# Odd mixer's gates and running maxima on quarters of the rows, MLP norms by an all-ones matmul, block-attention scores in another order

## What is computed

```python
x = first_block(x, ...)            # modulated rmsnorm, window attention + block ("moba") attention, MLP
for layer in range(2):
    h = _rmsnorm(x, mix_norm_g[layer])
    x = x + (_even_mixer(h) if layer == 0 else _odd_mixer(h))
    h = _rmsnorm(x, mlp_norm_g[layer])
    x = x + _sqrelu_mlp(h, mlp_w1[layer], mlp_w2[layer])   # relu(h @ w1)**2 @ w2

def _odd_mixer(h, ...):            # w_in is (1024, 3080): 512 q, 512 k, 1024 v, 1024 og, 8 gates
    p = h @ w_in
    qk = silu(causal_conv(p[..., :1024]))
    i_pre, f_pre = gates[..., :4] + i_b, gates[..., 4:] + f_b
    hc = _mlstm(q, k, v, i_pre, f_pre)      # 4 heads, logf = log_sigmoid(f_pre), cumulative sums,
    ...                                     # running maxima of i - cumsum(logf) per head and token
```

## Time and profile before

| | us |
|---|---|
| median of 3 runs | 1875.85 (1875.34 to 1876.64) |
| the profiled execution | 1876.47 |
| its span, first to last instruction | 1874.7 |
| PE busy | 1841.8 (98%) |
| DVE busy | 961.6 (51%) |
| ACT busy | 733.8 (39%) |

### The profile page before, as it was taken

How to read it: one execution, slowest core, us unless ns; L and a number is a source line. 1 busy time by engine, 2 the same in 40 slices (tenths; PEclk the granted TensorE clock), 3 DMA queues, 4 the chain that set the end, 5 groups by cost and what they waited for, 6 DMA issues and landing times.

```text
span 1874.7 us, 21068 instructions
## 1 busy us (share of the span) xinstructions
PE 1841.8 (98%) x8632; PEld 1497.2 (80%) x8632; DVE 961.6 (51%) x1389; ACT 733.8 (39%) x1043; POOL 39.1 (2%) x75
## 2 busy tenths in 40 slices
PE   5999999999999999999999999999999999999999
PEld 4787788788888888877888888888876788888887
DVE  7487546543434355767543434345735554444343
ACT  4355532332323243467442323243445443323231
POOL 0100000000000000001000000000011000000000
PEclk9999999899999999999999999999999999999999
DMA  8365543222222223211222222222220223222222
GB/s 330 117 198 186 168 163 120 88 101 90 101 90 101 97 95 118 79 35 46 90 91 101 90 101 101 90 102 90 90 79 36 78 90 111 92 101 91 101 90 79
DMA packets 55120, 197.65 MB, mean 105 GB/s; under 512 B 6400, under 2 KB 6656, under 8 KB 55024
## 3 DMA queue, kind: packets, MB, share of 16 engines
q1 hardware_dynamic: 52272, 188.24, 28.2%
q0 software_dynamic: 2320, 7.31, 1.4%
q10 hardware_dynamic: 432, 0.74, 0.1%
HBM read 194.13 MB, written 2.14 MB: 105 GB/s over the span
## 4 chain that ended last, share of the span: by engine, by line
PE 94%; DVE 4%; ACT 1%; issue 0%; DMA 0%; ACTq 0%; DVEq 0%
PE ps L314 27%; PE ps L316 26%; PE ps L315 26%; PE ps L350 2%; PE ps L351 2%; PE ps L352 2%; PE ps L439 1%; PE ps L815 1%; DVE ARENA L1384 1%; PE ps L722 1%; PE ps L368 1%; PE ps L682 1%; PE ps L520 0%; PE ps L802 0%; PE ps L494 0%
## 5 line engine op out<-in xcount | busy, mean ns | idle before, releaser
L314 PE MATMUL ps<-R0h,WH 128*128 128x512 f32 x1176 | 461.9, 393 | 5.9 <-DVE R0l L1436 4.6
L918 ACT ACTIVATE WH<-RAW 128x1024 fp32r<-128x1024 f32 x299 | 313.9, 1052 | 392.6 <-PE ps L316 337.7
L1377 DVE TENSOR_TENSOR WL<-RAW,WH 128x1024 fp32r<-128x1024 f32 x299 | 365.4, 1225 | 191.3 <-ACT WH L918 187.4
L315 PE MATMUL ps<-R0l,WH 128*128 128x512 f32 x1176 | 458.8, 390 | 0.0
L316 PE MATMUL ps<-R0h,WL 128*128 128x512 f32 x1176 | 458.8, 390 | 0.0
L314 PE MATMUL ps<-R1h,WH 128*128 128x512 f32 x1064 | 417.7, 393 | 3.0 <-DVE R1l L1588 2.5
L316 PE MATMUL ps<-R1h,WL 128*128 128x512 f32 x1064 | 414.7, 390 | 0.0
L315 PE MATMUL ps<-R1l,WH 128*128 128x512 f32 x1064 | 414.7, 390 | 0.0
L314 PEld LDWEIGHTS ps<-R0h,WH 128*128 128x128 f32 x1176 | 221.4, 188 | 57.6 <-DVE R0l L1436 6.4
L316 PEld LDWEIGHTS ps<-R0h,WL 128*128 128x128 f32 x1176 | 221.4, 188 | 46.4
L315 PEld LDWEIGHTS ps<-R0l,WH 128*128 128x128 f32 x1176 | 221.5, 188 | 45.3
(11 more groups left out here) (283 smaller groups left out, 1435.8 us busy)
## 6 DMA issues: line engine op xcount, KB each, us to landing
RAW<-in_W SPq DMA_DIRECT2D x339, 512.0 KB, 3.2
ARENA<-in_W SPq DMA_DIRECT2D x12, 512.0 KB, 13.2
XT<-in_X SPq DMA_DIRECT2D x4, 512.0 KB, 9.2
ARENA<-bias_scratch POOLq DMA_DIRECT2D x8, 256.0 KB, 4.3
XT<-in_X POOLq DMA_DIRECT2D x8, 256.0 KB, 3.5
out_x<-XT SPq DMA_DIRECT2D x8, 256.0 KB, 2.0
ARENA<-bias_scratch POOLq DMA_DIRECT2D x8, 128.0 KB, 3.6
con<-in_CON POOLq DMA_DIRECT2D x1, 578.0 KB, 4.3
```

Of the source, the lines that this page charges most:

```text
L314: e.matmul(ps(b), wh, hi, start=first, stop=False)
L315: e.matmul(ps(b), wh, lo, start=False, stop=False)
L918: e.activation(slot(n)[0], src, ACT.Copy).then_inc(sem["w_hi"])
L1377: e.tensor_tensor(wl, src, r32(wh), ALU.subtract).then_inc(sem["w_lo"])
```

## The change

- **Gates.** The chunk og8 goes (24 matmuls, one load of 512 KB, one split). The gate weights become 8 x 32 columns of `par` (wg), which grows from 164 to 421 columns, and are multiplied once by the norm's gain on DVE (`gate_weights`, one 128x256 operation before the residual sums of the even mixer). `gate_columns` multiplies them in plain fp32 with XT: 8 matmuls with 128 rows, 32 columns, 512 moving columns; k-step k writes the column quarter k mod 4 of bank 0. ACT copies the bank. `gate_sum`, one gemm later, adds the quarters with two 128x128 matmuls against 0/1 matrices, so that four copies of the 4 gate rows lie at partitions 0, 32, 64, 96. LI, FX and T2 are worked on with 128 partitions.
- **Maxima.** `gate_rows` takes head h from partitions 32h..32h+3, all four heads in a row, behind the v-gemm part that stood between them.
- **Pair of the odd mixer.** It now is the first two q/k chunks.
- **MLP norms (m1, m2).** `sums_wide` multiplies SQ by a 128x128 matrix of ones, 512 moving columns, at k-step 3. ACT takes the root of the 128x512 bank, DVE the reciprocal of 128x512. `bring` is gone there. One `hi` and one `lo` stand before the root, one behind.
- **Scores of the second kind.** Order of tiles (e,i): before 0,3 1,3 0,2 1,2 0,1 1,0 0,0 1,1; now 0,3 1,3 0,1 1,2 0,2 1,0 0,0 1,1, and the last waits for the third score instead of the fifth.

```diff
@@ scores, heads 4 to 7
-                    for b in (3, 5):
+                    for b in (7, 5):
                         open_bank(b)
+                    score(j, 0, 1)
+                    score(j, 1, 2)
+                    open_bank(3)
                     score(j, 0, 2)
-                    score(j, 1, 2)
-                    open_bank(7)
-                    score(j, 0, 1)
                     score(j, 1, 0)
                     score(j, 0, 0)
-                    e.wait_ge(sem["qk"], 8 * j + 5)
+                    e.wait_ge(sem["qk"], 8 * j + 3)
                     score(j, 1, 1)
@@ PE, norms of the MLPs
+            def sums_wide(i):
+                e.wait_ge(sem["ssq"], SSQ[i + 1])
+                open_bank(7)
+                e.matmul(ps(7), cc("ones"), SQ[:], start=True, stop=True).then_inc(sem["ss"])
...
-                            gemm([job, ((tag + "i", 1), WIDE[1], ("mlp_rr", MLP[tag] + 2))], x, ready, mid)
-                            bring(norm)
+                            gemm([job, ((tag + "i", 1), WIDE[1], ("mlp_rr", MLP[tag] + 2))], x, ready, mid, 3)
@@ PE, gates
-            def gate_rows(h):
-                b, at = (2, 3, 7, 6)[h], CC["sel"][0] + 128 * h
-                open_bank(b)
-                e.matmul(ps(b), con[0:4, at:at + 128], T2[0:4, :], start=True, stop=True).then_inc(sem["bc"])
+            def gate_rows():
+                for b in (2, 3, 7, 6):
+                    open_bank(b)
+                for h, b in enumerate((2, 3, 7, 6)):
+                    r = slice(32 * h, 32 * h + 4)
+                    e.matmul(ps(b), cc("sel")[r, :], T2[r, :], start=True, stop=True).then_inc(sem["bc"])
+            def gate_columns():
+                e.wait_ge(sem["wgs"], 1)
+                open_bank(0)
+                for k in range(KT):
+                    g, c0 = k % 4, COLS["wg"][0] + 32 * k
+                    t = e.matmul(PSB[0][32 * g:32 * g + 32, :], par[:, c0:c0 + 32], XT[:, k, :],
+                                 start=(k < 4), stop=(k > 3))
+                t.then_inc(sem["gcol"])
+            def gate_sum():
+                e.wait_ge(sem["gq"], 1)
+                for b, name in ((2, "sumi"), (3, "sumf")):
+                    open_bank(b)
+                    e.matmul(ps(b), cc(name), OG[:, 0, :], start=True, stop=True).then_inc(sem["gsum"])
@@ PE, odd mixer
-                gemm([(("og8", 0), 0, ("gt", 2)), (("oqk", 0), 1, ("c_rr", 1))], B, lambda k: ("flo", FOLD["m1"] + k + 1),
-                     lambda: sums(4))
+                gemm([(("oqk", OQK[o]), WIDE[1 + o], ("c_rr", o + 1)) for o in range(2)], B,
+                     lambda k: ("flo", FOLD["m1"] + k + 1), lambda: sums(4))
                 bring(4)
-                for o in range(1, 8):
+                gate_columns()
+                for o in range(2, 8):
                     gemm([(("oqk", OQK[o]), WIDE[(1 + o) % 4], ("c_rr", o + 1))], B)
+                    if o == 2:
+                        gate_sum()
@@ ACT and DVE, norms of the MLPs
-                                sqrt(NS[:, norm, 0:4], RS[norm] + 1)
-                                hi(2)
-                                bring(norm)
+                                hi()
+                                sqrt_wide(norm)
+                                hi()
...
-                                sums(norm)
-                                lo(2)
+                                lo()
+                                e.wait_ge(sem["sqrt"], NORM[norm] + 1)
+                                e.reciprocal(SQ[:], SQ[:]).then_inc(sem["rb"])
+                                lo()
                                 e.wait_ge(sem["rb"], BRING[norm])
```

More of the change, by code:

```diff
@@ L70, in chunk_plan @@
     plan += mlp("m1")
-    plan += [("og8", 0)] + [("oqk", n) for n in (0, 4, 1, 5, 2, 6, 3, 7)] + [("ov", c) for c in range(8)]
+    plan += [("oqk", n) for n in (0, 4, 1, 5, 2, 6, 3, 7)] + [("ov", c) for c in range(8)]
     plan += [("oo", n) for n in range(8)]
@@ L101 @@
 NORM = (0, 1, 2, 4, 5, 6)
-RS = (0, 2, 4, 12, 14, 16)
+RS = (0, 2, 4, 12, 12)
+SPREAD = {2: 3, 4: 5}
 SSQ = (0, 7, 13, 20, 27, 34, 41)
@@ L603, in mlp @@
             def mlp(tag, x, dst, ready, norm):
-                mid = None if norm is None else lambda: sums(norm)
+                mid = None if norm is None else lambda: sums_wide(norm)
                 for blk in range(4):
@@ L1569, in merge, with gate_weights @@
                         lo(2 if k == 1 else 1)
+            def gate_weights():
+                c0, (m0, m1) = COLS["wg"][0], COLS["mix1"]
+                w, g = blocks(par[:, c0:c0 + 256], 8), par[:, m0:m1]
+                e.tensor_tensor(w, w, bass.AP(g.tensor, g.offset, [g.ap[0], g.ap[1], [0, 32]]),
+                                ALU.mult).then_inc(sem["wgs"])
             def norm2():
@@ L1863, in gates @@
+                one = cc("ones")
                 e.wait_ge(done, 7)
-                e.wait_ge(sem["gx"], 2)
-                e.tensor_tensor(t2r, t2r, fx, ALU.add).then_inc(done)
-                one = cc("ones")[0:4, :]
+                e.tensor_tensor_scan(FX, bass.AP(one.tensor, one.offset, [one.ap[0], [0, S]]), T2, 0.0, ALU.mult,
+                                     ALU.subtract).then_inc(done)
                 e.wait_ge(done, 8)
-                e.tensor_tensor_scan(fx, bass.AP(one.tensor, one.offset, [one.ap[0], [0, S]]), t2r, 0.0, ALU.mult,
-                                     ALU.subtract).then_inc(done)
+                e.tensor_tensor(LI, LI, FX, ALU.subtract).then_inc(done)
@@ L2069, in constants @@
     for h in range(4):
-        con[h, 768 + 128 * h:896 + 128 * h] = 1.0
-    con[:, 1280:1408] = np.where(i[:, None] < i[None, :], 0.0, NEG)
-    con[:, 1408], con[:, 1410] = 1.0, 1.0
+        con[33 * h, 768:896] = 1.0
+    con[:, 896:1024] = np.where(i[:, None] < i[None, :], 0.0, NEG)
+    con[:, 1024], con[:, 1026] = 1.0, 1.0
+    same = i[None, :] % 32 < 4
+    con[:, 1028:1156] = same & (i[:, None] % 32 == i[None, :] % 32)
+    con[:, 1156:1284] = same & (i[:, None] % 32 == i[None, :] % 32 + 4)
     dist = np.arange(640) - 127
@@ L2147 @@
     setp("convw", v["od_conv_w_2"][0].reshape(4, 8, 128).transpose(2, 1, 0).reshape(128, 32))
-    par[0:4, COLS["ib"][0]] = v["od_i_b_2"][0]
-    par[0:4, COLS["fb"][0]] = v["od_f_b_2"][0]
+    setp("wg", wg.reshape(8, 128, 32).transpose(1, 0, 2).reshape(128, 256))
+    setp("eps", EPS)
+    for g in range(0, P, 32):
+        par[g:g + 4, COLS["ib"][0]] = v["od_i_b_2"][0]
+        par[g:g + 4, COLS["fb"][0]] = v["od_f_b_2"][0]
     con, oh = constants()
```

78 lines of the change are left out of this document (41 added, 37 removed).

## The result

| | before | after |
|---|---|---|
| median of 5 runs, us | 1876.08 (1875.34 to 1876.64) | **1868.18** (1867.06 to 1868.65) |
| the profiled execution | 1876.47 | 1868.18 |
| its span | 1874.7 | 1866.4 |

A forecast was written before the change was run, and what follows sets the result against it. PE was taken to bound the kernel (94% of the chain that ended last). The terms summed to -7.2, -7.1 before rounding: 1876.47 to 1869.4, less 0.6 for the median 1868.8, range 1867.4 to 1870.0 (wider: 1867.0 to 1873.0).

The forecast's parts named there:

- steps 1 to 4: Odd mixer's gates: chunk dropped -5.44, columns on quarters +1.8, two sum matmuls +2.0, added DVE work free.
- steps 5 and 10: Gate rows of the odd mixer: quarters together plus a wait for ACT's copy, -1.7; clock no longer falls, -1.65.
- step 6: Norms of m1 and m2: all-ones matmul of 1.17 us replaces sums and spread, -0.63 each, -1.3 in all.
- step 7: Norms of m1 and m2: 3.4-us reciprocal makes the sixth chunk's split late, +0.3 in m1, 0 in m2.
- step 8: Scores, four pairs of heads: new order gains 0.4 of 0.57 us each, -1.6 (bounds -0.8 and -2.3).
- step 9: Kernel start: load of `par` grows by 128 KB, its delay paid in full, +0.4 (bounds 0 and 1.6).
- the estimate of 8.3 ns: Rival at the MLP norms: reciprocal takes 4.4 us, m1 +1.0, m2 +0.6, 1870.4; chance 0.13, shared with similar late operands.

The follow-up runs named there:

- e2: Changed kernel with all eight k-steps of the gate columns on one column quarter, copy and sums taking 32 rows: 1872.62 us.
- e4: Changed kernel with gate rows as before, all from partitions 0 to 3, two ahead of the v-gemm part and two behind: 1871.36 us.
- e7: Changed kernel with one v-gemm part moved between the gate rows and the first head's matmuls: 1866.29 us.
- e6: Changed kernel with the root ahead of ACT's first weight split and the reciprocal ahead of DVE's first, in m1 and m2: 1868.03 us.
- e8: Changed kernel with a second 128x512 reciprocal into scratch ahead of the first, in m1 and m2: 1876.10 us.
- e11: Changed kernel with the new score order, but the last score waiting for the fifth score instead of the third: 1869.19 us.
- e1: Kernel before with only the new order of the scores and its earlier wait: 1874.70 us.
- e5: Changed kernel with all four gate rows from partitions 0 to 3, in one block at their new place: 1873.23 us.

## Why the prediction was right

The forecast of 1868.8 was 0.6 us off, inside its own range, and part of that closeness is luck. The sum was 1.2 us off: it gave 1869.4 for the profiled execution, which took 1868.18. The 0.6 us that I took off for the median held for the kernel before; of the changed kernel the median and the profiled execution are the same. Between the profiled executions the sum was -7.1 and -8.3 came: scores, norms and `par` gave 0.5, 0.6 and 0.45 more, and the norm ahead of the first MLP took 0.6 that no term had.

- **Gate chunk, columns, sums (steps 1 to 4): right in mechanism, and to the hundredth by luck.** 1.85 us where 1.8 was said, no wait for the copy, and the sum of the three is -1.64 as forecast. But in it two misses cancel. With the changes between whole array and quarters on both sides of them the columns cost some 2.05 us: spread and columns take 2.95 from 1299.80 to the second gemm matmul behind them, less that one matmul, and the spread alone took 0.90 before. The sums cost 1.72 and not 2.0 (1308.22 to 1310.17, less one matmul): 0.86 each, with nothing to add for going in and out of fp32. The quarters run side by side in full; e2 shows what in turn would have cost, 5.1 us.
- **Gate rows and clock (steps 5 and 10): right together, -3.47 for -3.35.** Rows 1.14 and wait 0.76 against 2.1 in all. e4 gives the two back, with the clock, and e7 shows the 0.76 to be the copy's, by hiding it.
- **MLP norms (step 6): the mechanism right, the term too small.** The all-ones matmul costs 0.86 us in the stream, not 1.17: it starts at 942.56 and the second gemm matmul behind it at 943.65, less the 0.23 of one gemm matmul. I had added 0.3 for going in and out of fp32, but 0.87 a matmul already held it here. That makes -0.93 to -1.0 a norm for -0.63.
- **The late split (step 7): right.** The reciprocal took 3.35 us for 3.4; PE waited some 0.4 for 0.3 in m1 and not at all in m2, where some 0.6 us were to spare for 0.4. e6 and e8 tie the wait to this reciprocal. The Trainium skill (VectorE: DVE Perf Modes, First, the fixed hardware budget) has a repeat count of 8 for a reciprocal, which read as eight cycles an element was the estimate of 8.3 ns; the 512 elements took 6.5 ns each.
- **Scores (step 8): too small by 0.5.** I kept 0.17 us of each pair for the last score standing behind its neighbour. The full 0.53 came, and e11 puts all of it on the wait for the fifth score.
- **`par` (step 9): nothing where +0.4 was said,** which was its lower bound. DVE started 0.25 us earlier, within what its start varies by from one execution to the next, and the chain no longer begins with `par`.
- **What had no term: the norm ahead of the first MLP.** Its half-clock stretch is in both kernels, and what it costs varies by over a microsecond between executions. The changed kernel had 1.3 us more of gemms under it in its profile, which took 0.6 of the gain. I read one profile and took its clock as given.

## What to carry to other kernels

Work on a quarter of the rows or columns of the array is worth spreading over all four quarters, even at the price of a matmul or two that adds the copies: in plain fp32 the time falls by nearly four, and a clock fall behind few-row matmuls goes with it. The order within the quarters was free with two such matmuls in a row for each, and cost with four in a row; three were not tried. Look at the granted clock wherever PE waits: the price of a wait includes the gemms behind it at half clock, 1.7 us behind the 3.0-us wait of e8. Matmuls of constants in the two waits of the first MLP's norm (1.8 and 2.5 us) bought back 3.1 us in one execution and 2.1 in another. And where a stretch at half clock differs in length between executions, read more than one before a microsecond is put down to an edit.

## What the runs showed of the hardware

- Two plain fp32 matmuls in a row on one column quarter don't hold back those of another; four in a row do (eight matmuls take 1.95 us in pairs on four quarters, 5.37 with four in a row on two, where 3.5 would be the full overlap, and 7.05 on one). The starts fit four records under way for each quarter.
- A full 7 us on 32 columns of 128 rows left the clock at 1.00; 1.96 us on 4 rows right behind the transposes were followed by 3.4 us at 0.50 in three kernels (before, e1, e4), and in e5 the clock fell within 4.2 us on 4 rows, while 1.98 us on 4 rows behind a v-gemm part were not.
- Behind one 3.0-us wait of PE the clock was at 0.50 for 3.4 us; at the two waits of the first MLP's norm it was there for 6.8 us in three executions and for 10.2 in nine.
- A load of 210 KB instead of 82 was there no later: the first instruction that uses it starts at 8.17 to 8.67 us in twelve executions with the larger, at 8.39 and 8.45 in two with the smaller.
- Plain fp32 matmuls of 32 or 64 rows between 128-row gemms cost 0.38 us a pair more than those of 128 rows.
